# A two-layer decoder trunk on one core: the order of the output projection's blocks, of the work on VectorE between two stages, and of the first phase

## The chip, the core and the metric

The kernel runs on one core of a Trainium2 chip. The core has a matrix engine (TensorE; PE in the profile, with its weight loads on PEld), VectorE (DVE), ScalarE (ACT), GpSimd (POOL), and SyncE (SP), which here only issues DMAs. They run side by side and meet at semaphores. SBUF is the on-chip memory, and PSUM (eight banks of 128 x 512 fp32) takes the matmul results. The metric is the device time of one execution in microseconds (us), lower is better.

## The reference, cut to what matters

One sequence of 512 positions with 1024 features passes through two layers; every array is fp32.

```
c_act = silu(c)
for layer in (0, 1):
    sh_m, sc_m, g_m, sh_f, sc_f, g_f = split(c_act @ ada_w[layer] + ada_b[layer], 6)
    hm = x * (1 + sc_m) + sh_m
    y  = mixer(hm)                        # layer 0: gated linear attention + mLSTM
                                          # layer 1: stick-breaking + dilated window attention
    x  = layer_norm(RES_ALPHA * x + (1 + g_m) * y,  ln_g[layer, 0], ln_b[layer, 0])
    hf = x * (1 + sc_f) + sh_f
    yf = (silu(hf @ w1) * (hf @ w3)) @ w2
    x  = layer_norm(RES_ALPHA * x + (1 + g_f) * yf, ln_g[layer, 1], ln_b[layer, 1])

# end of layer 0's mixer
hb = sigmoid(ob) * head_norm(mlstm(...), ml_g)
y  = concatenate([oa, hb]) @ w_out        # (512 x 1024) @ (1024 x 1024)
```

## The kernel before

**Products.** A product in fp32 is made of three: each operand is split in a high part (`h_hi`, `w_hi`) and the rest (`h_lo`, `w_lo`), and PE adds up hi\*lo, hi\*hi and lo\*hi in PSUM. The weights come as slots of 128 x 1024, 512 KB each, numbered through the program: 0 to 5 the first phase, then the other projections of layer 0, 29 to 36 the output projection `out0`, 37 to 80 the up and gate projections of the first feed-forward stage `ffn0`, then its down projection, and layer 1 in the same way. SP loads slot s into `raw[s % 4]`; ACT makes `w_hi` (L738), POOL makes `w_lo` (L692), and in the first phase DVE makes it (L1862). `w_hi` and `w_lo` have four places each as well (`RING` = `RAW` = 4). ACT starts slot s when PE is done with slot s - 4 (`slot_done`), SP when POOL or DVE is done with the `w_lo` of slot s - 4. The input's high part is ACT's work (L752, L934), its low part DVE's (L1784, L2138). The high part of a chunk is made of `tmp`, which DVE (L2066, L2131) or ACT (L767) writes.

**adaLN vectors.** They are six blocks of 1024 for each layer, and run beside the products. For a block, DVE adds up eight scaled slots of `ada_w` in `ada_acc` (L1797 the first, L1800 the other seven, in `ada_block`), and PE adds over the partitions with eight matmuls one column wide (`ada_cols`). The slots come through two buffers `ada_raw`; SP issues slot i when DVE is done with slot i - 2, and `ADA_BESIDE` says behind which weight slot it does so. Block 4, the scale of ffn0's input, is wanted before ffn0 starts.

**First phase.** The shift and scale of layer 0's input come in four pieces of 256 columns (p = 0 to 3). For each, DVE adds up a part in `first_block` (L1847, L1850) and PE takes the rest itself (`FIRST_ON_PE`) and adds over the partitions (`first_cols`, L1321). DVE adds the bias (`first_mod`, L1857 and L1858), ACT scales two chunks of x (L767), and PE takes these in the products va and qa (L1332 to L1334). The whole phase loads `ada_first`, x and six weight slots.

**out0.** The concatenated input has eight chunks of 128 features: 0 to 3 of the linear attention, 4 to 7 of the mLSTM, which are last. For each of these four, ACT scales the head's numerator (L914), DVE multiplies it with the gate (`ml_gate`, L2059), PE transposes it (`turn_in`, L1501), DVE scales it into `tmp` (`cat_tmp`, L2066), ACT makes `h_hi`, DVE `h_lo` (`cat_lo`, L1784). The output has four blocks of 128 positions, two banks each; the transposes use banks 4 and 5, which are block 2's. PE does blocks 0, 3 and 1 with chunks 0 to 3, then block 2 with chunks 0 to 3, which frees the places of slots 29 to 32, then for each block in turn chunks 4 to 7 (L1131 to L1133).

**Between two stages** (`norm`). For each block DVE adds the residual (L2165, L2166), takes statistics (L2170 to L2175), and ACT normalizes (L947). PE transposes two blocks at a time into banks (`turn`, L1115), and these halves of 256 positions go chunk by chunk through `half_chunks`: DVE L2131, ACT L934, DVE L2138. The next stage's first products are done by halves: half 0 on all of a step's units, then half 1. When both halves are through, DVE also scales the normalized x with gain and bias (`affine`, L2205 and L2206, two instructions of 128 x 1024 a block), for the residual that comes later.

**ffn0** takes slots in steps of four (two of `w1`, two of `w3`). In every step DVE has the products of up and gate (L2235, then the low part of the hidden state) and two instructions on an `ada_w` slot for each of four slots of its two buffers (the loop on SP issues a weight slot and an ada slot in turn). Layer 1 opens with the projections qc and kc, whose results DVE takes out of PSUM in `qk_panel` (L2280).

Each engine runs its instructions strictly in the order in which they are written.

## Time and profile before

| | |
|---|---|
| time, median of 3 runs | 1407.68 us (1406.48 to 1409.59) |
| the profiled execution's own time | 1406.98 us |
| its span in the trace | 1405.2 us |
| PE busy | 1343.3 us (96%), 6558 matmuls |
| DVE, ACT, POOL busy | 619.5 (44%), 456.8 (33%), 507.5 (36%) |
| granted TensorE clock, mean | 0.98 |
| DMA | 173.81 MB, 124 GB/s on average, 332 GB/s in the first fortieth |

A row of the profile is one instruction or a few of one kind: start in us from the span's start, busy us, engine, line of the kernel, operation, output and inputs with their shapes, how many (x), and in brackets how long the engine stood still before it and what it waited for. Busy shares are averages over stages which differ in what they wait for.

### The profile page before, as it was taken

The page shows a single profiled execution, that of the slowest core. Times are in us where ns is not written, and L with a number is a line of the kernel's source. Part 1 is how long each engine was busy: PE and PEld are TensorE (multiplying, and loading weights), DVE is VectorE, ACT ScalarE, POOL GpSimd, SP SyncE. Part 2 cuts the span into 40 slices and gives each one's busy share as a digit, 9 for nine tenths or more (in the row PEclk, how much of TensorE's full clock was granted, in tenths as well). Part 3 has the DMA queues.
Part 4 walks back from the last instruction along what each step waited for, and adds up shares of the span by engine and source line. Part 5 has one row for each costly group of instructions (what it writes and reads, how often), then busy time and mean ns, then how long its engine had stood idle before and what let it go on. Part 6 is the DMA issues. An engine that isn't in the chain of part 4 may idle for free.

```text
span 1405.2 us, 17072 instructions
## 1 busy us (share of the span) xinstructions
PE 1343.3 (96%) x6558; PEld 1111.4 (79%) x6558; DVE 619.5 (44%) x842; ACT 456.8 (33%) x622; POOL 507.5 (36%) x209
## 2 busy tenths in 40 slices
PE   7999999889999999999899999988989999999996
PEld 6778877778888888888788777878888888887885
DVE  4489657578534343300884323347692101100006
ACT  3343254333232332112322344316243323232112
POOL 0243222323453444344235122220254444444444
PEclk9999999999999999999999899999999999999998
DMA  9972546522555465643325421112023322234312
GB/s 332 165 150 80 190 135 121 180 76 98 191 190 195 163 218 173 183 129 96 119 80 191 113 90 53 42 57 76 30 91 108 101 91 103 90 103 137 90 60 60
DMA packets 93538, 173.81 MB, mean 124 GB/s; under 512 B 15736, under 2 KB 61960, under 8 KB 93357
## 3 DMA queue, kind: packets, MB, share of 16 engines
q1 hardware_dynamic: 90344, 169.63, 39.1%
q10 hardware_dynamic: 3140, 3.43, 0.9%
q8 instruction: 39, 0.64, 0.2%
q14 instruction: 15, 0.11, 0.0%
HBM read 170.87 MB, written 4.52 MB: 125 GB/s over the span
## 4 chain that ended last, share of the span: by engine, by line
PE 68%; issue 19%; POOL 6%; DVE 4%; ACT 1%; DMA 1%; SPq 0%; POOLq 0%; DVEq 0%; ACTq 0%
PE ps L1099 13%; PE ps L1100 13%; PE ps L1101 13%; POOL w_lo L692 6%; PE ps L1131 6%; PE ps L1132 6%; PE ps L1133 6%; PE ps L1614 1%; PE ps L1274 1%; PE ps L1275 1%; PE ps L1276 1%; PE ps L1642 1%; PE ps L1625 1%; PE ps L1629 1%; PE ps L1288 1%
## 5 line engine op out<-in xcount | busy, mean ns | idle before, releaser
L692 POOL TENSOR_TENSOR w_lo<-raw,w_hi 128x1024 fp32r<-128x1024 f32 x197 | 488.3, 2484 | 857.1 <-ACT w_hi L738 856.7
L1099 PE MATMUL ps<-h_lo,w_hi 128*128 128x512 f32 (+2 forms) x1064 | 402.0, 378 | 15.1 <-DVE h_lo L2138 5.9
L1100 PE MATMUL ps<-h_hi,w_hi 128*128 128x512 f32 (+2 forms) x1064 | 398.1, 374 | 0.0
L1101 PE MATMUL ps<-h_hi,w_lo 128*128 128x512 f32 (+2 forms) x1064 | 397.8, 374 | 0.0
L738 ACT ACTIVATE w_hi<-raw 128x1024 fp32r<-128x1024 f32 x203 | 213.2, 1057 | 483.9 <-PE ps L1133 177.0
L1099 PEld LDWEIGHTS ps<-h_lo,w_hi 128*128 128x128 f32 (+1 forms) x1064 | 203.8, 192 | 55.1 <-issue 8.4
L1101 PEld LDWEIGHTS ps<-h_hi,w_lo 128*128 128x128 f32 (+1 forms) x1064 | 203.7, 191 | 35.4
L1100 PEld LDWEIGHTS ps<-h_hi,w_hi 128*128 128x128 f32 (+1 forms) x1064 | 204.2, 192 | 34.2
L2235 DVE TENSOR_TENSOR tmp<-tmp,ps 128x512 f32<-128x512 f32 x44 | 30.1, 688 | 261.4 <-PE ps L1101 261.4
L1131 PE MATMUL ps<-w_hi,hid_lo 128*128 128x512 f32 x344 | 136.8, 398 | 1.8 <-issue 0.9
L1133 PE MATMUL ps<-w_lo,hid_hi 128*128 128x512 f32 x344 | 136.8, 398 | 0.0
L1132 PE MATMUL ps<-w_hi,hid_hi 128*128 128x512 f32 x344 | 136.7, 397 | 0.0
L2165 DVE TENSOR_TENSOR ps<-ps,gate_ffn 128x1024 f32<-128x1024 f32 x7 | 8.6, 1230 | 192.2 <-PE ps L1133 192.2
L1131 PEld LDWEIGHTS ps<-w_hi,hid_lo 128*128 128x128 f32 x344 | 65.1, 189 | 18.1 <-issue 1.3
L2254 DVE SCALAR_TENSOR_TENSOR ada_acc<-ada_raw,c_act,ada_acc 128x1024 f32<-128x1024 f32 x35 | 58.3, 1666 | 44.6 <-DMA ada_raw<-astream 44.2
L1133 PEld LDWEIGHTS ps<-w_lo,hid_hi 128*128 128x128 f32 x344 | 65.0, 189 | 15.6
L1132 PEld LDWEIGHTS ps<-w_hi,hid_hi 128*128 128x128 f32 x344 | 65.0, 189 | 15.6
L1800 DVE SCALAR_TENSOR_TENSOR ada_acc<-ada_raw,c_act,ada_acc 128x1024 f32<-128x1024 f32 x35 | 62.5, 1786 | 23.7 <-DMA ada_raw<-astream 21.2
L990 ACT ACTIVATE hid_hi<-tmp 128x512 f32 (+1 forms) x44 | 27.7, 633 | 92.3 <-DVE tmp L2235 92.2
L1274 PE MATMUL ps<-w_hi,h_lo 128*128 128x512 f32 (+1 forms) x128 | 48.0, 375 | 0.0
L1275 PE MATMUL ps<-w_hi,h_hi 128*128 128x512 f32 (+1 forms) x128 | 46.9, 367 | 0.0
L1276 PE MATMUL ps<-w_lo,h_hi 128*128 128x512 f32 (+1 forms) x128 | 46.8, 366 | 0.0
(276 smaller groups left out, 1586.3 us busy)
## 6 DMA issues: line engine op xcount, KB each, us to landing
raw<-wstream SPq DMA_DIRECT2D x205, 512.0 KB, 4.0
ada_raw<-astream SPq DMA_DIRECT2D x80, 512.0 KB, 4.3
ada_first<-astream SPq DMA_DIRECT2D x16, 256.0 KB, 6.8
ada_first<-astream SPq DMA_DIRECT2D x8, 512.0 KB, 10.5
ln_rows<-row_scratch SPq DMA_DIRECT2D x3, 1024.0 KB, 6.7
skew_scratch<-f_scratch ACTq DMA_DIRECT2D x1, 2304.0 KB
xa<-xT SPq DMA_DIRECT2D x4, 512.0 KB, 8.5
out<-xa SPq DMA_DIRECT2D x3, 512.0 KB, 3.5
```

Of the source, the lines that this page charges most:

```text
L692: nc.gpsimd.tensor_tensor(w_lo[:, slot, :], raw[:, slot % RAW, :], w_hi[:, slot, :].bitcast(F32), ALU.subtract).then_inc(sem("w_lo_ready"), 1)
L738: nc.scalar.activation(w_hi[:, slot, :], raw[:, slot, :], ACT.Copy).then_inc(sem("w_hi_ready"), 1)
L1099: pe.matmul(o, w_h, x_l, start=start, stop=False)
L1100: pe.matmul(o, w_h, x_h, start=False, stop=False)
L1101: return pe.matmul(o, w_l, x_h, start=False, stop=stop)
L1131: pe.matmul(o, x_lo, w_h, start=k == 0, stop=False)
L1132: pe.matmul(o, x_hi, w_h, start=False, stop=False)
L1133: m = pe.matmul(o, x_hi, w_l, start=False, stop=k == nk - 1)
L1274: pe.matmul(o, h_lo[:, k, tokens], w_hi[:, s % RING, w], start=start, stop=False)
L1275: pe.matmul(o, h_hi[:, k, tokens], w_hi[:, s % RING, w], start=False, stop=False)
L1276: m = pe.matmul(o, h_hi[:, k, tokens], w_lo[:, s % RING, w], start=False, stop=stop)
L1800: V.scalar_tensor_tensor(ada_acc[:], src, c_act[:, k:k + 1], ada_acc[:], ALU.mult, ALU.add).then_inc(sem("ada_step"), 1)
```

## The change

- **out0.** Four more pairs of buffers hold `w_hi` and `w_lo` of slots 33 to 36, in columns of the arena that the mLSTM has left by then. PE does blocks 0, 3 and 1 with chunks 0 to 3 as before, then finishes block 0 and block 1 with chunks 4 to 7; `ada_cols(4)` follows; then block 2 with all eight chunks, the transposes of blocks 0 and 1, and block 3's chunks 4 to 7. The scheme is the one that `out1` had already, and shares its code now. ACT makes `w_hi` of slot 33 right after the scaling of the mLSTM's heads, and of 34, 35, 36 behind `h_hi` of chunks 5, 6 and 7. Slots 37 to 40 wait for places 29 to 32, which PE leaves in block 2.
- **adaLN block 4 in out0.** DVE's last four slots of it came behind all of the chunks' work; now 4 and 5 come behind `ml_gate(1)`, 6 and 7 between `cat_tmp(7)` and `cat_lo(6)`. SP issues the loads of 6 and 7 (ada slots 36 and 37 are its 4 and 5) as `ADA_BESIDE` says.
- **Norm 0 on ACT.** `w_hi` of ffn0's first slots comes before the second and third normalization.
- **Turn of half 1 before ffn0.** It stands behind the second step unit of half 0, and stood behind the first.
- **Scaling of x.** Before ffn0 and ffn1 two blocks are scaled early and two behind ffn's first step. Before layer 1 all four are scaled behind `qk_panel("kc1")`.
- **First phase.** DVE makes `h_lo` of a piece's first chunk (for p = 0) and `w_lo` of slot 1 ahead of the reduction for piece 1, and the other slots' `w_lo` behind a whole reduction. PE calls `first_cols(p + 1)` ahead of the products of chunks 1, 3 and 5, and did so between the two products of a chunk. One slot of piece 3 moves from DVE to PE.

```diff
-    FIRST_ON_PE = ((0, 1, 2, 3), (7,), (7,), ())
+    FIRST_ON_PE = ((0, 1, 2, 3), (7,), (7,), (7,))
...
-                  29: (26, 27), 30: (28, 29), 31: (30, 31), 32: (32, 33), 34: (34, 35), 36: range(36, 40)}
+                  29: (26, 27), 30: (28, 29), 31: (30, 31), 32: (32, 33), 34: (34, 35), 35: (36, 37), 36: (38, 39)}
...  ACT, out0
         hi_until(out0 + 4)
         for h in range(1, 4):
             ml_scaled(h)
+        hi_until(out0 + 5)
         for n in range(4, KC):
             hi_of_chunk(H_BASE["cat0"] + n, n)
+            if n >= 5:
+                hi_until(out0 + n + 1)
...  ACT, norm
             normalize(0)
-            normalize(1)
...
             n0 = SLOTS[following][0]
-            hi_until(n0 + 1)
+            if i == 0:
+                hi_until(n0 + 2)
+            normalize(1)
+            hi_until(n0 + (4 if i == 0 else 1))
             normalize(2)
...  PE, the first units of ffn
-                        if i == 2 and hf == 0 and q == 1 and u == 0:
+                        if i != 1 and hf == 0 and q == 1 and u == 0:
                             turn(i, 1)
-                    if i != 2 and hf == 0 and q == 0:
+                    if i == 1 and hf == 0 and q == 0:
                         turn(i, 1)
...  PE, first phase
-                if k == 5:
-                    first_cols(3)
+                if k % 2 and p < 3:
+                    first_cols(p + 1)
...
-                    if k % 2 and p < 2 and part is (first_qa if k % 4 == 3 else first_va):
-                        first_cols(p + 1)
...  PE, out0, behind blocks 0, 3 and 1 with chunks 0 to 3
-            pe.wait_ge(sem("h_tmp_ready"), H_BASE["cat0"] + KC)
-            for k in range(4):
-                rows_of(2, k).then_inc(sem("slot_done"), 1)
+        for tb in range(2):
+            for k in range(4, KC):
+                if tb == 0:
+                    slot_waits(OUT[0] + k)
+                    pe.wait_ge(sem("h_ready"), H_BASE["cat0"] + k + 1)
+                m = out_row(0, tb, k)
+            m.then_inc(sem("y_full"), 1)
+        pe.wait_ge(sem("r_ready"), 1)
+        ada_cols(4, 1)
+        pe.wait_ge(sem("h_tmp_ready"), H_BASE["cat0"] + KC)
+        for k in range(KC):
+            m = out_row(0, 2, k)
+            if k < 4:
+                m.then_inc(sem("slot_done"), 1)
+        m.then_inc(sem("y_full"), 1)
+        turn(0, 0)
+        for k in range(4, KC):
+            out_row(0, 3, k).then_inc(sem("slot_done"), 1)
...  DVE, norm and ffn
-            for tb in range(TB):
+            early = 0 if i == 1 else 2
+            for tb in range(early):
                 affine(tb, ln_rows2, sem("x_row"))
...
+            def rest():
+                for tb in range(early, TB):
+                    affine(tb, ln_rows2, sem("x_row"))
...
             step(0, True)
+            rest()
...
         qk_panel("kc1")
+        rest1()
```

Below, rows of instructions stand as the two programs have them, one engine at a time.

DVE in the first phase, before: from the first piece's bias (L1857) to the second's. L1847 and L1850 are the reduction, L1784 is `h_lo`, L1862 `w_lo`.

```order
L1857 TENSOR_TENSOR mod<-ps,vec 128x2
L1858 TENSOR_TENSOR scl<-ps,scale_b_74 128x2
L1847 TENSOR_SCALAR ada_acc<-ada_first,c_act 128x512
L1850 SCALAR_TENSOR_TENSOR ada_acc<-ada_first,c_act,ada_acc 128x512
L1784 TENSOR_TENSOR h_lo<-tmp,h_hi 128x512
L1862 TENSOR_TENSOR w_lo<-raw,w_hi 128x1024
L1850 SCALAR_TENSOR_TENSOR ada_acc<-ada_first,c_act,ada_acc 128x512
L1784 TENSOR_TENSOR h_lo<-tmp,h_hi 128x512
L1850 SCALAR_TENSOR_TENSOR ada_acc<-ada_first,c_act,ada_acc 128x512 x2
L1862 TENSOR_TENSOR w_lo<-raw,w_hi 128x1024
L1850 SCALAR_TENSOR_TENSOR ada_acc<-ada_first,c_act,ada_acc 128x512 x2
```

DVE there, after (L1873 the bias, L1863 and L1866 the reduction, L1800 `h_lo`, L1878 `w_lo`):

```order
L1873 TENSOR_TENSOR mod<-ps,vec 128x2
L1874 TENSOR_TENSOR scl<-ps,cols 128x2
L1800 TENSOR_TENSOR h_lo<-tmp,h_hi 128x512
L1878 TENSOR_TENSOR w_lo<-raw,w_hi 128x1024
L1863 TENSOR_SCALAR ada_acc<-ada_first,c_act 128x512
L1866 SCALAR_TENSOR_TENSOR ada_acc<-ada_first,c_act,ada_acc 128x512 x2
L1800 TENSOR_TENSOR h_lo<-tmp,h_hi 128x512
L1866 SCALAR_TENSOR_TENSOR ada_acc<-ada_first,c_act,ada_acc 128x512 x4
L1878 TENSOR_TENSOR w_lo<-raw,w_hi 128x1024
```

Two instructions of the reduction stood between the scale and the first `h_lo`, and one more between two of the `w_lo`s; now nothing stands ahead of the first `h_lo`, and the reduction for the next piece begins behind the first `w_lo`.

DVE in out0, before: from `ml_gate(0)` (L2059) to the last of block 4 (L1800). L2066 is `cat_tmp`, L1784 `cat_lo`.

```order
L2059 TENSOR_TENSOR og<-og,num 128x4x128 x2
L2066 TENSOR_SCALAR tmp<-ps,vec 128x512
L2059 TENSOR_TENSOR og<-og,num 128x4x128
L2066 TENSOR_SCALAR tmp<-ps,vec 128x512
L2059 TENSOR_TENSOR og<-og,num 128x4x128
L1784 TENSOR_TENSOR h_lo<-tmp,h_hi 128x512
L2066 TENSOR_SCALAR tmp<-ps,vec 128x512
L1784 TENSOR_TENSOR h_lo<-tmp,h_hi 128x512
L2066 TENSOR_SCALAR tmp<-ps,vec 128x512
L1784 TENSOR_TENSOR h_lo<-tmp,h_hi 128x512 x2
L1800 SCALAR_TENSOR_TENSOR ada_acc<-ada_raw,c_act,ada_acc 128x1024 x4
```

DVE there, after (L2074 `ml_gate`, L1816 block 4, L2081 `cat_tmp`, L1800 `cat_lo`):

```order
L2074 TENSOR_TENSOR og<-og,num 128x4x128 x2
L1816 SCALAR_TENSOR_TENSOR ada_acc<-ada_raw,c_act,ada_acc 128x1024 x2
L2081 TENSOR_SCALAR tmp<-ps,vec 128x512
L2074 TENSOR_TENSOR og<-og,num 128x4x128
L2081 TENSOR_SCALAR tmp<-ps,vec 128x512
L2074 TENSOR_TENSOR og<-og,num 128x4x128
L1800 TENSOR_TENSOR h_lo<-tmp,h_hi 128x512
L2081 TENSOR_SCALAR tmp<-ps,vec 128x512
L1800 TENSOR_TENSOR h_lo<-tmp,h_hi 128x512
L2081 TENSOR_SCALAR tmp<-ps,vec 128x512
L1816 SCALAR_TENSOR_TENSOR ada_acc<-ada_raw,c_act,ada_acc 128x1024 x2
L1800 TENSOR_TENSOR h_lo<-tmp,h_hi 128x512 x2
```

Two instructions of block 4 stand ahead of the first `cat_tmp` now, and two ahead of the last two `cat_lo`.

DVE at the start of layer 1, before: the last two scalings of x (L2205, L2206), then the eviction of qc (L2280).

```order
L2205 TENSOR_TENSOR xa<-xa,ln_rows_79 128x8x128
L2206 TENSOR_TENSOR xa<-xa,ln_rows_79 128x8x128
L2205 TENSOR_TENSOR xa<-xa,ln_rows_79 128x8x128
L2206 TENSOR_TENSOR xa<-xa,ln_rows_79 128x8x128
L2223 MEMSET cols 128x1
L2280 TENSOR_SCALAR qc<-ps 128x512 x2
L2285 COPY f_rows<-ps 4x1152
L1806 TENSOR_TENSOR mod<-ps,vec 128x8
L1797 TENSOR_SCALAR ada_acc<-ada_raw,c_act 128x1024
```

DVE there, after: the last low parts of the input (L2154), the eviction of qc and kc (L2303), block 10's sums and those of the next (L1822, L1813, L1816), then the scaling (L2221, L2222).

```order
L2154 TENSOR_TENSOR h_lo<-tmp,h_hi 128x256 x3
L2303 TENSOR_SCALAR qc<-ps 128x512 x2
L2308 COPY f_rows<-ps 4x1152
L1822 TENSOR_TENSOR mod<-ps,vec 128x8
L1813 TENSOR_SCALAR ada_acc<-ada_raw,c_act 128x1024
L1816 SCALAR_TENSOR_TENSOR ada_acc<-ada_raw,c_act,ada_acc 128x1024 x3
L2303 TENSOR_SCALAR kc<-ps 128x512
L1816 SCALAR_TENSOR_TENSOR ada_acc<-ada_raw,c_act,ada_acc 128x1024 x4
L2303 TENSOR_SCALAR kc<-ps 128x512
L2221 TENSOR_TENSOR xa<-xa,ln_rows_78 128x8x128
L2222 TENSOR_TENSOR xa<-xa,ln_rows_78 128x8x128
L2221 TENSOR_TENSOR xa<-xa,ln_rows_78 128x8x128
```

All eight instructions of the scaling stood ahead of qc's eviction (six of them above the rows shown here or at their start), and stand behind kc's now.

## Rows read from the trace of the kernel before

**Rows 1.** A stretch: width; busy us PE, PEld, DVE, ACT, POOL; clock, DMA, GB/s.

```profile
1100.00:1150.00 50.00, 50.00 (x222) 41.42 (x221) 5.34 (x8) 15.60 (x20) 21.56 (x9) 1.00 0.33 105
```

**Rows 2.** Stretch 0 to 35, and instructions in time order: start, busy, engine, [idle].

```profile
0.00:35.00 35.00, 24.57 (x104) 21.42 (x105) 17.42 (x30) 11.99 (x15) 0.20 (x4) 1.00 0.98 332
...
15.45 0.63 ACT L752 ACTIVATE h_hi<-tmp 128x512 fp32r<-128x512 f32 x1
...
16.25 0.49 DVE L1847 TENSOR_SCALAR ada_acc<-ada_first,c_act 128x512 f32<-128x512 f32 x1 [1.68 <-DMA ada_first<-astream]
...
18.18 0.79 PE L1332 MATMUL ps<-w_hi,h_lo 128*128 128x512 f32 x1 [3.88 <-DVE h_lo L1784]
...
32.26 0.50 PE L1332 MATMUL ps<-w_hi,h_lo 128*128 128x512 f32 x1 [1.07 <-DVE h_lo L1784]
...
48.61 1.02 PE L1321 MATMUL ps<-ones,ada_acc 128*128 128x1 f32 x8 [1.97 <-DVE ada_acc L1850]
```

**Rows 3.** The timeline of out0 on ACT, POOL and PE.

```profile
262.13 1.06 ACT L738 ACTIVATE w_hi<-raw 128x1024 fp32r<-128x1024 f32 x1 [3.09 <-PE ps L1133]
...
263.26 9.01 POOL L692 TENSOR_TENSOR w_lo<-raw,w_hi 128x1024 fp32r<-128x1024 f32 x3 [14.19 <-ACT w_hi L738]
...
269.08 0.47 PE L1131 MATMUL ps<-w_hi,h_lo 128*128 128x512 f32 x1 [1.58 <-issue]
...
272.38 0.47 PE L1131 MATMUL ps<-w_hi,h_lo 128*128 128x512 f32 x1 [1.67 <-issue]
...
274.70 0.47 PE L1131 MATMUL ps<-w_hi,h_lo 128*128 128x512 f32 x1 [0.70 <-issue]
...
290.28 1.86 PE L1115 MATMUL ps<-cst,xa 128*128 128x128 f32 x15 [1.10 <-ACT xa L947]
```

**Rows 4.** The timeline of ACT, DVE and POOL in out0 and behind it.

```profile
246.87 4.35 ACT L914 ACTIVATE num<-num,cols,rstd 128x128 f32<-128x128 f32 x11
...
248.17 1.45 DVE L2059 TENSOR_TENSOR og<-og,num 128x512 f32<-128x512 f32 x1 [1.50 <-ACT num L914]
...
259.68 1.28 DVE L1800 SCALAR_TENSOR_TENSOR ada_acc<-ada_raw,c_act,ada_acc 128x1024 f32<-128x1024 f32 x1
...
264.30 2.45 DVE L1800 SCALAR_TENSOR_TENSOR ada_acc<-ada_raw,c_act,ada_acc 128x1024 f32<-128x1024 f32 x1 [1.96 <-DMA ada_raw<-astream]
...
312.40 1.45 DVE L2131 TENSOR_SCALAR tmp<-ps,scl,bia 128x256 f32<-128x256 f32 x3 [1.99 <-PE ps L1115]
...
312.72 2.39 POOL L692 TENSOR_TENSOR w_lo<-raw,w_hi 128x1024 fp32r<-128x1024 f32 x1 [4.72 <-ACT w_hi L738]
...
313.77 1.62 DVE L2138 TENSOR_TENSOR h_lo<-tmp,h_hi 128x256 fp32r<-128x256 f32 x1
```

**Rows 5.** The start of ffn0 on PE, and the stretch in which its clock was halved.

```profile
299.71 0.39 PE L1099 MATMUL ps<-h_lo,w_hi 128*128 128x256 f32 x1 [2.09 <-DVE tmp L2131]
...
302.76 0.58 PE L1099 MATMUL ps<-h_lo,w_hi 128*128 128x256 f32 x1 [2.05 <-DVE h_lo L2138]
...
303.00:307.00 4.00, 4.00 (x19) 3.93 (x20) 3.97 (x10) 1.99 (x4) 2.36 (x1) 0.50 0.77 262
...
311.75 0.44 PE L1115 MATMUL ps<-cst,xa 128*128 128x128 f32 x2 [1.47 <-ACT xa L947]
```

**Rows 6.** DVE and PE around the second step of ffn0.

```profile
330.71 0.40 PE L1099 MATMUL ps<-h_lo,w_hi 128*128 128x512 f32 x1
...
338.75 0.75 DVE L2257 TENSOR_SCALAR ada_acc<-ada_raw,c_act 128x1024 f32<-128x1024 f32 x1
...
348.09 0.47 PE L1099 MATMUL ps<-h_lo,w_hi 128*128 128x512 f32 x1 [0.87 <-POOL w_lo L692]
```

**Rows 7.** The start of layer 1 on DVE and PE, and the stretch behind it.

```profile
725.31 0.69 DVE L2280 TENSOR_SCALAR qc<-ps 128x512 f32<-128x512 f32 x1
...
726.10 0.76 PE L1099 MATMUL ps<-h_lo,w_hi 128*128 128x512 f32 x1 [2.27 <-issue]
...
726.00:730.00 4.00, 3.90 (x9) 3.13 (x10) 3.86 (x5) 0.00 (x0) 0.00 (x0) 0.50 0.09 24
```

153 lines of the change are left out of this document (76 added, 77 removed).

## The prediction, made before the changed kernel was run

> **What bounds the kernel now.** I read the page's first part, then windows of 50 us, then the list of waits of PE, then PE's timeline at every pause. PE is busy for 96% of the span, and in a stretch between two stages without a pause: 222 matmuls of 512 columns in 50.00 us, or 0.225 us each, at the full clock, while DVE has 5.34 us of work and POOL 21.56 [rows 1]. Other engines matter only where PE stands still, so each edit is worth what it does to one of PE's pauses. Those within its reach are three in the first phase [rows 2], four in out0 [rows 3], three at the start of ffn0 [rows 5], one a step later [rows 6], and one at the start of layer 1 [rows 7]. Two of these twelve are followed by a stretch at a granted clock of 0.50, the lower of TensorE's two levels (1.2 against 2.4 GHz) [rows 5, 7].
>
> **First phase.** PE's first product waits 3.88 us, for a `h_lo` [rows 2]. ACT has the high part ready at 15.45 + 0.63 = 16.08, but DVE has a reduction ahead, and that waits 1.68 us for its DMA until 16.25. In the new order `h_lo` comes first: 16.08 + 0.69 + 0.1 to start, so PE begins at 16.9 instead of 18.18, a gain of 1.3. The waits of 1.07 and 1.97 [rows 2] are of the same kind (the second is for the last piece's reduction on DVE, which is one instruction shorter and is asked for no earlier than before), and I take both away. PE pays for four more tiny products of its own and their weight loads, some 0.8 by the eight of 48.61 at 1.02 us. Sum: -1.3 - 1.1 - 2.0 + 0.8 = -3.5. Bounds: the DMA is at 0.98 of its time here, 332 GB/s [rows 2]. If the pieces land only when DVE took them, the waits of 1.07 and 1.97 come back under another name and only the start is left, -1.3 + 0.8, with part of one wait about -1.0. If the four small products are free, -4.1. I take -3.5: both waits name DVE as the releaser, and not the DMA.
>
> **out0: what goes.** PE waits 1.58, 1.67 and 0.70 for `w_lo` of slots 34 to 36. ACT can't begin them before places 29 to 32 are free at 262.13, and POOL then takes three at 3.0 each [rows 3]. With buffers of their own they don't wait for PE. The 1.10 ahead of the transposes [rows 3] waits for the normalized block 1. Block 1 is now done a whole block (48 matmuls, 10.9 us) ahead of these, so it goes. Together 5.05.
>
> **out0: what comes.** I lay DVE's new order on the old times. `ml_gate(1)` ends at 248.17 + 1.45 = 249.6. Slots 4 and 5 of block 4, 1.28 each [rows 4], last until 252.2. ACT is through with the heads at 246.87 + 4.35 = 251.2 and makes `w_hi` of slot 33, so POOL is busy from 252.4 to 254.8. Here the trace shows how the two engines meet: a DVE instruction with two inputs in SBUF stands still while POOL works. `h_lo` of 128 x 256 took 1.62 at 313.77, to just behind the end of POOL's (312.72 + 2.39 = 315.11), and a block 4 instruction 2.45 in place of 1.28. The three with a PSUM input beside that same POOL instruction took 1.45 together, 0.48 each, and were not held [rows 4]. The Trainium skill has this as a rule ("SBUF — State Buffer", "SBUF: two separate sides"): the shared port pair is an exclusive lock for the whole instruction, and with two SBUF inputs VectorE needs it. By that rule the extra wait below comes; were the ports shared evenly, DVE would be through about 5 us sooner and there would be none.
> With that, and 0.7 for `cat_tmp` or `cat_lo` (the like eviction of 128 x 512 took 0.69 [rows 7]): `cat_tmp(4)` to 252.9, `ml_gate(2)` held to 255.4, `cat_tmp(5)` 256.2, `ml_gate(3)` 256.9, `cat_lo(4)` 257.5, `cat_tmp(6)` 258.3. POOL takes slot 34 from 258.0 to 260.4, so `cat_lo(5)` ends at 261.0 and `cat_tmp(7)` at 261.8. Slot 35 goes from 261.0 to 263.4; block 4's slot 6 is held and ends at 264.7, then POOL has slot 36 until 267.1, slot 7 ends at 268.3, and `cat_lo(6)` at 269.0.
> PE is through with chunks 0 to 3 of three blocks at about 261.6 (1.0 later than now, since the last transpose waits for `ml_gate(3)`), does chunks 4 and 5 of block 0 (six matmuls, 1.36 us each), and wants chunk 6 at 264.3. It waits 4.8. I add 2.1 for a stretch at the lower clock behind so long a pause: behind 2.27 and behind 2.09 and 2.05 the clock was 0.50 for four us and more [rows 5, 7], where each us holds half of the work. Sum: +6.9 - 5.05 = +1.9. Bounds: no wait at all, -5.05; one more of POOL's splits in DVE's way, 2.4, a wait of 7.2 and the clock, +4.3. The moved DMAs cost nothing: ada slots 36 to 39 are issued one weight slot sooner, with their landings ahead of the times above. The four `w_hi` are on ACT between chunks, 1.06 each, and ACT was idle for 3.09 there [rows 3].
>
> **ffn0's start.** Today 2.09, 2.05 and 1.47 [rows 5]. The first two come of splits that lie among the chunks of half 0: POOL holds `h_lo`, and ACT has a `w_hi` between two `h_hi`. Now these four slots are split before the second and third normalization. The four us from 303 at clock 0.50 did the work of two [rows 5], and go with them: -2.0. So 7.6 goes. In its place PE comes earlier to the transposes of half 1, which want the last normalized block: a wait of about 1.4, like the 1.47 now. The chunks' own pace (one `tmp` and one `h_lo`, 0.48 + 0.41, against 1.36 per chunk on PE, but with the first two in a row) costs 0.7. Net -5.5; bounds -8.3 (none of the new waits) and 0 (all come back, since DVE arrives late from out0).
> **A step later** PE waits 0.87 for slot 44 [rows 6]. SP's loop issues weight and ada slots in turn, and the ada slot needs DVE. DVE's first of block 5 ends at 339.5, 8.8 behind the start of PE's second step at 330.71 [rows 6]. Now DVE has step 0 at once, 2.6 us, then four scalings, at least 1.28 each and one or two held by POOL for another 1.2, so that it is 10.1 behind: +1.3. Bounds 0 to 2.5. What the six instructions taken away ahead of step 0 give is nothing, as PE didn't wait for them.
> The wait for chunk 6 pushes everything, so from out0 to slot 44 it is +1.9 - 5.5 + 1.3 = -2.3.
>
> **Layer 1's start.** PE waits 2.27 at 726.10 since bank by bank it needs qc out of PSUM, which DVE does at 725.31 [rows 7], behind eight scalings of x at 1.2 us or more. They go behind kc now: -2.3. If the clock of 0.50 behind it (3.90 us of four [rows 7]) stays up too, -4.4. If something else of DVE's is as late, 0. I take -2.3, since a chunk pause before it can drop the clock as well. The scalings meet POOL's splits later and delay the eviction of vc by some 0.5, for which nobody waits for long. Norm 2 and ffn1 have no pause of this kind, the loop of POOL unrolled around slot 33 has the same instructions, so both are 0.
>
> **The sum**: -3.5 - 2.3 - 2.3 = -8.1, on the profiled execution's 1406.98 (1.8 of it outside the span of 1405.2, which stay): 1398.9. The median is 0.7 higher, so 1399.6.
>
> **Rivals.**
> A. *No wait in out0.* DVE's last low parts come in time, because POOL's splits start later or earlier than I have them and miss the long instructions. For: the hold is an accident of a few tenths. Against: the two instructions of block 4 are 2.6 us even unheld, ahead of a chunk wanted in 2.7. Price: -6.9 and some of the one at slot 44 back: about 1393.
> B. *The first phase is bound by its DMAs.* For: 0.98 busy [rows 2]. Against: of the waits only DVE's own was for a DMA. Price: the first phase gives 1.0 instead of 3.5: 1402.
> C. *Little changes.* The new wait in out0 is at its upper bound (+4.3 for +1.9), and half of what ffn0 wins comes back: 1399.6 + 2.4 + 2.8 = 1404.8, and up to 1408 if layer 1's start gives nothing.
> D. *Slower.* SP's queue in ffn0: each weight slot is behind an ada slot that waits for DVE, and DVE takes step j only when PE has done it. If DVE is late once, the weights are late, PE is late and nothing makes up for it. This decides when DVE's first of block 5 ends more than about 11 us behind the start of the second step: then a split as late as slot 44's, 2.5 a time, comes in each of five turns, +12, to 1411. For: the 0.87 is there [rows 6], and it gets worse. Against: behind it DVE has waited for its DMAs, not they for it.
>
> **How the numbers follow.** Forecast 0.50, A 0.20, B 0.15, C 0.10, D 0.05. The forecast's own range is 1396 to 1402.5. The range for 8 in 10 takes in most of A, all of B, and the lower part of C: 1391.5 to 1404.5. The measurement tells 0.2% (2.8 us) from no change: faster is below 1404.9, which is the forecast, A, B and half of C, 0.85 with a little off for what I haven't seen; same 0.10; slower, D, 0.05.
>
> **What would show it.** First phase: PE's first product at 16.9 and no pause up to out0; a pause whose releaser is a DMA speaks for B. out0: no wait for `w_lo` of 34 to 36, but one of 4 to 5 us ahead of block 0's third late chunk, with `h_lo` as releaser, two instructions of block 4 of about 2.4 in front of it, and the clock down behind it. ffn0: half 0 without a pause of 2 us and at clock 1.0; about 2.2 at slot 44. Layer 1: qc's eviction some 9 us earlier. The forecast is wrong if PE goes through out0 without a pause (A), or if the mean wait of ffn0's later steps is not zero (D).

## The result, and the profile after

The changed kernel takes 1387.72 us (median of 4 runs, 1384.56 to 1391.53), the kernel before 1408.47 beside it. The ratio is 0.9851, 95% interval 0.9836 to 0.9867: 20.8 us faster. The forecast was 1399.6, 8.1 faster, with a range down to 1391.5, so the measured time lies below the range. The direction was right, the size was wrong by more than a factor of two.

The profiled execution has a span of 1382.7 us; it is the fastest of the four. These are the places that the forecast named, in PE's timeline (start, busy, engine, in brackets the pause ahead and what it waited for):

```profile
16.63 0.80 PE L1340 MATMUL ps<-w_hi,h_lo 128*128 128x512 f32 x1 [2.55 <-DVE h_lo L1800]
...
23.91 1.05 PE L1329 MATMUL ps<-ones,ada_acc 128*128 128x1 f32 x8 [0.76 <-DVE ada_acc L1866]
...
263.33 0.76 PE L1546 MATMUL ps<-out_hi,h_lo 128*128 128x512 f32 x1 [3.86 <-DVE h_lo L1800]
...
338.77 0.47 PE L1114 MATMUL ps<-h_lo,w_hi 128*128 128x512 f32 x1 [1.56 <-POOL w_lo L695]
...
710.55 0.80 PE L1114 MATMUL ps<-h_lo,w_hi 128*128 128x512 f32 x1
```

The 3.88 of the first product is 2.55 now [rows 2]. The pauses of 1.07 and 1.97 are gone, with one of 0.76 in their place. In out0 the three for `w_lo` and the 1.10 [rows 3] are gone, and 3.86 stands ahead of block 0's third late chunk. Between it and 338.77, where three stood [rows 5], the timeline has 0.17 and 0.27. At slot 44 there is 1.56 for 0.87 [rows 6], and the last row, the counterpart of 726.10 [rows 7], has no pause.

Here are three windows of the changed kernel and two of the one before (columns: busy us of PE, PEld, DVE, ACT, POOL with their instructions, then PE's clock, the DMAs' share, GB/s). The first of before and of after lie in down0, the second in down1, the third of after in ffn1. After:

```profile
570.00:620.00 50.00, 50.00 (x222) 41.42 (x221) 1.60 (x4) 9.54 (x9) 23.10 (x10) 1.00 0.53 110
1290.00:1340.00 50.00, 50.00 (x222) 41.40 (x221) 0.00 (x0) 9.54 (x9) 22.61 (x10) 1.00 0.27 85
1100.00:1150.00 50.00, 50.00 (x222) 41.42 (x221) 5.34 (x8) 14.63 (x18) 22.81 (x10) 1.00 0.30 95
```

Before:

```profile
570.00:620.00 50.00, 50.00 (x215) 40.23 (x215) 7.89 (x7) 9.56 (x9) 21.50 (x10) 1.00 0.56 147
1290.00:1340.00 50.00, 50.00 (x216) 40.25 (x216) 0.00 (x0) 9.55 (x9) 21.24 (x9) 1.00 0.32 95
```

This is the surprise. PE is busy without a pause at the full clock in all five, and still does 215 or 216 matmuls in the down projections of before and 222 in those of after, as many as everywhere else [rows 1]. From the start of one matmul to the start of the next it is 0.2333 us in the one and 0.2267 in the other.

Where the time went in the two profiled executions, by the start of the same matmul in both:

| up to the end of | before | after | this stage, after less before |
|---|---|---|---|
| first phase | 73.61 | 68.95 | -4.7 |
| layer 0's mixer up to out0 | 241.29 | 236.71 | +0.1 |
| out0, start of ffn0, up to slot 44 | 348.09 | 338.77 | -4.7 |
| ffn0 | 559.55 | 550.27 | 0.0 |
| down0 | 686.56 | 672.52 | -4.8 |
| norm 1 and qc | 726.10 | 710.55 | -1.5 |
| layer 1's mixer, out1 | 1021.64 | 1001.83 | -4.3 |
| ffn1 | 1267.92 | 1248.18 | +0.1 |
| down1, end | 1405.2 | 1382.7 | -2.7 |

The forecast had the first, third and sixth line, 8.1 in all; they hold 10.9. It had 0 for down0, layer 1's mixer and down1, and these hold 11.8.

### The profile page after: what moved, and what is told of

It is laid out like the page before. It is cut to its first block, busy times and chain, and to the rows that moved or that the text cites. A ratio compares the mean times of both kernels' runs of the same rounds, so it can differ in the third digit from the quotient of the medians.

```text
span 1382.7 us, 17078 instructions
## 1 busy us (share of the span) xinstructions
PE 1332.4 (96%) x6566; PEld 1109.4 (80%) x6566; DVE 615.0 (44%) x841; ACT 457.4 (33%) x622; POOL 507.3 (37%) x209
## 4 chain that ended last, share of the span: by engine, by line
PE 81%; issue 7%; DVE 7%; POOL 3%; ACT 2%; DMA 0%; DVEq 0%; SPq 0%; POOLq 0%; ACTq 0%
PE ps L1114 15%; PE ps L1115 15%; PE ps L1116 14%; PE ps L1146 5%; PE ps L1148 5%; PE ps L1147 5%; POOL w_lo L695 2%; PE ps L1282 2%; PE ps L1283 2%; PE ps L1284 2%; PE ps L1643 1%; PE ps L1671 1%; PE ps L1296 1%; PE ps L1250 1%; PE ps L1252 1%
## 5 line engine op out<-in xcount | busy, mean ns | idle before, releaser
L695 POOL TENSOR_TENSOR w_lo<-raw,w_hi 128x1024 fp32r<-128x1024 f32 x193 | 477.5, 2480 | 826.7 <-ACT w_hi L747 826.4
L747 ACT ACTIVATE w_hi<-raw 128x1024 fp32r<-128x1024 f32 x199 | 208.9, 1057 | 486.3 <-DMA raw<-wstream 167.2
L1148 PE MATMUL ps<-w_lo,hid_hi 128*128 128x512 f32 x344 | 133.9, 389 | 0.0
L1147 PE MATMUL ps<-w_hi,hid_hi 128*128 128x512 f32 x344 | 133.8, 389 | 0.0
L2278 DVE SCALAR_TENSOR_TENSOR ada_acc<-ada_raw,c_act,ada_acc 128x1024 f32<-128x1024 f32 x35 | 58.9, 1684 | 44.8 <-DMA ada_raw<-astream 44.5
L1816 DVE SCALAR_TENSOR_TENSOR ada_acc<-ada_raw,c_act,ada_acc 128x1024 f32<-128x1024 f32 x35 | 57.4, 1639 | 24.1 <-DMA ada_raw<-astream 21.5
L1283 PE MATMUL ps<-w_hi,h_hi 128*128 128x512 f32 (+1 forms) x128 | 46.7, 365 | 0.0
L1284 PE MATMUL ps<-w_lo,h_hi 128*128 128x512 f32 (+1 forms) x128 | 46.7, 365 | 0.0
```

Of the source, the lines that this page charges most:

```text
L695: nc.gpsimd.tensor_tensor(w_lo[:, slot, :], raw[:, slot % RAW, :], w_hi[:, slot, :].bitcast(F32), ALU.subtract).then_inc(sem("w_lo_ready"), 1)
L747: nc.scalar.activation(w_hi[:, slot, :], raw[:, slot, :], ACT.Copy).then_inc(sem("w_hi_ready"), 1)
L1147: pe.matmul(o, x_hi, w_h, start=False, stop=False)
L1148: m = pe.matmul(o, x_hi, w_l, start=False, stop=k == nk - 1)
L1283: pe.matmul(o, h_hi[:, k, tokens], w_hi[:, s % RING, w], start=False, stop=False)
L1284: m = pe.matmul(o, h_hi[:, k, tokens], w_lo[:, s % RING, w], start=False, stop=stop)
```

## The experiments

Times are medians in us. The kernel before ran beside every one of these kernels and took 1407.0 to 1408.7; the ratio is to it, with a 95% interval. A difference to the changed kernel is one of medians, to its 1387.72 where nothing else is said. The interval given with some of them is worked out from both ratios.

**Where the arena lies.** The arena is the part of SBUF, laid out last, in which `hid`, the hidden state of the feed-forward stages, and the mixers' buffers lie. The change puts the vector `scale_b1`, 32 bytes per partition that lay ahead of the arena, in free columns of `cols`, and so moves all of the arena from byte 137120 to 137088:

```diff
-    scale_b1 = at("scale_b1", [P, KC])
...
+    scale_b1 = cols[:, 5, 0:KC]
```

Two kernels turn that one thing.

```diff
+    place[0] += 32
     arena = place[0]
```

In the kernel before:

> The kernel before with 32 unused bytes ahead of the arena, so that its start goes from 137120 (32 above a multiple of 64) to 137152 (a multiple of 64); no instruction is moved. Theory 'place': the change dropped a 32-byte vector ahead of the arena and so put hid_hi and hid_lo, the stationary tiles of the down projections, on multiples of 64 bytes; that alone takes the matmul spacing of down0 and down1 from 0.2333 us to 0.2268, 528 matmuls each, 6.9 us in all, and perhaps a few us more in layer 1, whose tensors lie in the arena too: 6 to 12 us faster than before. Rival 'order': the spacing is a consequence of the new order (other engines' work beside the down projections), and then this kernel keeps 0.2333 and stays within 0.2% of before.

1407.73, ratio 0.9994 (0.9984 to 1.0004), spacing 0.2333. In the changed kernel:

> The changed kernel with 32 unused bytes ahead of the arena, which puts its start back at 137120. Theory 'place': spacing in the down projections 0.2333 again, and the time some 7 to 12 us over the changed kernel's 1387.7, about 1395 to 1399; what is left against before is what the new order brings, by the pauses of the trace 4.7 in the first phase, 4.7 from out0 to slot 44 and about 1 at layer 1's start. Rival 'order': the spacing stays 0.2268 and the time stays at 1387 to 1389.

1393.73, ratio 0.9901 (0.9879 to 0.9922), spacing 0.2333 again:

```profile
570.00:620.00 50.00, 50.00 (x216) 40.24 (x215) 2.27 (x5) 9.15 (x10) 21.77 (x9) 1.00 0.51 119
```

So it is the place and not the order: no instruction differs from the changed kernel, and it costs 6.0 us (interval 3 to 11). But it is not multiples of 64, as the kernel before with the pad shows. The next three look for the rule. The first moves hid, the stationary operand of the down projections (the one that is loaded as weights), by 8 columns, the second the arena by 96 bytes, and the third hid by 24 columns.

```diff
-    hid_hi = ar("hid_hi", [P, FC, S], 0, F32R)
-    hid_lo = ar("hid_lo", [P, FC, S], FC * S, F32R)
+    hid_hi = ar("hid_hi", [P, FC, S], 8, F32R)         # 24 and 56 in others
+    hid_lo = ar("hid_lo", [P, FC, S], FC * S + 8, F32R)
```

> The kernel before with hid_hi and hid_lo alone set 8 columns (32 bytes) further on in the arena, so that only they lie on multiples of 64 bytes. Theory 'stationary tile': the down projections go at 0.2268 and the gain is their 6.9 us. Rival 'whole arena': part of the gain of the first run comes from other tensors (the attention of layer 1, the evictions into the arena); then this one gains clearly less than that. Rival 'order': no gain.

1408.30, ratio 1.0004 (0.9991 to 1.0016).

> The kernel before with 96 unused bytes ahead of the arena: its start goes from 137120 to 137216, a multiple of 128, where 137152 (a multiple of 64 only) had brought nothing. The changed kernel's arena starts at 137088, a multiple of 128 too. Theory 'place, by 128': the down projections' matmul spacing goes from 0.2333 us to 0.2267, 528 in each of two stages, 6.9 us, and the kernel is 0.4 to 0.6% faster than before with no instruction moved. Rival 'absolute place': it is the arena's lower start, or how it stands to another tensor, and this one stays at 0.2333 and at the time of before.

1408.07, ratio 0.9989 (0.9974 to 1.0005), 0.2333 in down0 and 0.2323 in down1.

> The kernel before with only hid_hi and hid_lo 24 columns (96 bytes) further on, which puts these two on a multiple of 128. Theory 'stationary tile': spacing 0.2267 in the down projections and the same gain as with the whole arena moved. Rival 'more than hid': no change of spacing, or a gain clearly smaller than that of the moved arena.

1407.07, ratio 0.9988 (0.9972 to 1.0004), 0.2324 in both. With the first pad these are four misses: remainders of 192 (twice) and 0 (twice) of 256 are as slow as before's 160, or nearly. A remainder of 128 was left:

> The kernel before with hid_hi and hid_lo 56 columns (224 bytes) further on: their start is 137344, which leaves 128 when divided by 256. So far the slow starts were 137120, 137152 and 137216 (remainders 160, 192 and 0), and the fast ones 137088 in the changed kernel and 32896 of h_hi, the stationary tiles of ffn's neighbour out0 (remainder 128 both). Theory 'remainder 128 of 256': spacing in the down projections 0.2267 and 0.3 to 0.5% faster than before, with no instruction moved. Rival 'something else of the changed arena': 0.2333 and no gain.

1402.62, ratio 0.9956 (0.9942 to 0.9970), down0 and down1 as in the changed kernel:

```profile
570.00:620.00 50.00, 50.00 (x223) 41.38 (x222) 8.78 (x8) 10.53 (x10) 22.20 (x9) 1.00 0.65 165
1290.00:1340.00 50.00, 50.00 (x222) 41.39 (x222) 0.00 (x0) 9.54 (x9) 22.25 (x10) 1.00 0.30 95
```

That is 6.1 us from 224 bytes per partition, with no instruction moved. `w_hi`, the moving operand there, and `h_hi`, the stationary one of out0 and the moving one of ffn0, lie at 82048 and 32896, remainder 128 both. Is it each place, or one against the other? For that `w_hi` and `w_lo`, and with them all that lies behind, are moved by 128 bytes:

```diff
+    place[0] += 128
     w_hi = at("w_hi", [P, RING, SLOT], F32R)
```

> The kernel before with 128 unused bytes ahead of w_hi (w_hi, w_lo and all behind them 128 bytes further on: w_hi at 82176, remainder 0 of 256) and hid_hi and hid_lo 24 columns further on in the arena, at 137344 (remainder 128). The moving operand w_hi and the stationary operand then differ by 128 in the remainder. Theory 'absolute place of the stationary tile': spacing 0.2267 in the down projections. Rival 'place of the two operands against each other': 0.2333 there, and in out0, where h_hi (remainder 128) is stationary and w_hi moves, over 0.2267 as well. Rival 'neither' as in the run before: 0.2333 in the down projections only.

> The kernel before with w_hi and w_lo 128 bytes further on (remainder 0 of 256) as in the run that went at 0.2325 everywhere, and with hid_hi and hid_lo at 137472, remainder 0 too. Theory 'the same remainder': the down projections go at 0.2267, and ffn (w at 0, h at 128) at 0.2325. Rival 'each at 128 by itself': 0.2325 or 0.2333 in both.

The first took 1422.73 in its one run, the second 1415.70 in its one. Their windows in ffn0 and down0 follow. For comparison, ffn0 in the kernel before:

```profile
400.00:450.00 50.00, 50.00 (x230) 41.67 (x229) 21.97 (x21) 13.61 (x17) 19.84 (x8) 1.00 0.49 172
```

With `w_hi` at remainder 0 and hid at 128:

```profile
400.00:450.00 50.00, 50.00 (x225) 40.89 (x224) 17.84 (x18) 14.02 (x17) 21.39 (x9) 1.00 0.48 168
590.00:640.00 50.00, 50.00 (x216) 40.51 (x216) 1.60 (x4) 9.54 (x9) 21.40 (x10) 1.00 0.52 121
```

With hid at remainder 0, like `w_hi`:

```profile
400.00:450.00 50.00, 50.00 (x225) 40.84 (x225) 18.74 (x18) 14.14 (x17) 22.26 (x10) 1.00 0.47 168
590.00:640.00 50.00, 50.00 (x222) 41.44 (x221) 1.61 (x4) 9.55 (x9) 22.64 (x10) 1.00 0.52 113
```

Down0 is back at 222 matmuls with both operands at 0. In ffn0, where `w_hi` at 0 meets h at 128, a matmul of 512 columns comes every 0.2324 us in both, and every 0.2269 in the kernel before (some one-column matmuls stand in these windows too). So what counts is whether stationary and moving operand start at the same remainder of 256 bytes.

The changed kernel's own out0 agrees. Of its four new pairs of buffers that of slot 33 begins at remainder 128, like `h_hi`, and the high parts of slots 34 to 36 at 192. In block 2, at the full clock, the six matmuls with slot 33 (from 281.47 on) start 0.2266 us apart, those with slot 34 0.2322, with 35 0.2288 and with 36 0.2303. With the pad of 32 bytes the six of slot 33 are at 0.2334 as well. Two things are open: why 64 bytes cost less here than in down0, and why hid at 137216 gave 0.2333 in down0 with the arena moved and 0.2324 with hid alone moved.

**The first phase undone** in the changed kernel (`FIRST_ON_PE`, the place of `first_cols` and DVE's order as in the diff's minus lines).

> The changed kernel with the first phase of before (the slots on PE, the place of first_cols, the order on DVE). The forecast priced the new first phase at 3.5 us, the profiles of before and after show 4.7 by the start of the linear attention: so 3.5 to 4.7 us slower than the changed kernel. Rival: a start that is late by 4 is swallowed later, since the pauses behind it depend on DMAs and not on PE: under 1.5.

1393.03, ratio 0.9886 (0.9856 to 0.9916): 5.3 over the changed kernel (interval 0.2 to 9.7), and the three pauses are back:

```profile
17.87 0.79 PE L1340 MATMUL ps<-w_hi,h_lo 128*128 128x512 f32 x1 [3.48 <-DVE h_lo L1802]
...
31.47 0.50 PE L1340 MATMUL ps<-w_hi,h_lo 128*128 128x512 f32 x1 [1.05 <-DVE h_lo L1802]
...
47.80 1.02 PE L1329 MATMUL ps<-ones,ada_acc 128*128 128x1 f32 x8 [1.93 <-DVE ada_acc L1868]
```

They were DVE's and not the DMAs', which ends rival B. The traces narrow the price. From PE's first product to its short wait for `w_lo` at the start of the next stage (67.96 before, 63.30 after) it is 46.7 to 47.0 us in all nine profiles with the new first phase, and 49.6 to 51.5 in all eleven with the old one. The long ones among these are seven in which the clock is at 0.50 for 3.4 us behind the third pause. The old order in the changed kernel is one of the seven, the kernel before is not.

**Layer 1's scaling undone**:

```diff
-            early = 0 if i == 1 else 2
+            early = 4 if i == 1 else 2
```

> The changed kernel with all four scalings of x ahead of layer 1's first projections, where they stood before. The forecast gave their move 2.3 us (0 to 4.4). The wait of 2.27 ahead of the second projection's first matmul comes back, and the time is about 2 us over the changed kernel's, 1389.7. Rival: 0, since qc's eviction waits for something else now; or 4.4 with a stretch at clock 0.50.

1392.08, ratio 0.9883 (0.9869 to 0.9898): 4.4 more (interval 1.5 to 7.5). The pause is back:

```profile
716.12 0.76 PE L1114 MATMUL ps<-h_lo,w_hi 128*128 128x512 f32 x1 [2.11 <-issue]
```

The 2.3 of the forecast lies inside. In the trace the stretch from the last wait for a normalized block (687.05 in the changed kernel) to the wait for `sb_a` in the mixer (777.60) is 92.0 us here for 90.5 in the changed kernel, so the pause itself is worth about 1.5.

**Norm 0 undone**, with out0 kept:

```diff
-            if i == 0:
-                hi_until(n0 + 2)
             normalize(1)
-            hi_until(n0 + (4 if i == 0 else 1))
+            hi_until(n0 + 1)
...
-                        if i != 1 and hf == 0 and q == 1 and u == 0:
+                        if i == 2 and hf == 0 and q == 1 and u == 0:
...
-            early = 0 if i == 1 else 2
+            early = (4, 0, 2, 2)[i]
```

> The changed kernel with norm 0 as before (order of w_hi and normalization on ACT, transposes of half 1 behind the first unit, all four scalings of x ahead of ffn0's first step), and with out0 as changed. The forecast gave this place 5.5 us, and the profile of the changed kernel shows no pause there. If norm 0's order brings it, the pauses of 2.09, 2.05 and 1.47 come back, and the time is 4 to 7 us over the changed kernel's, about 1393. Rival: out0's new order brings it, since slots 37 to 40 get their places earlier and block 1 its normalization; then the time rises by under 2 us.

1396.72, ratio 0.9906 (0.9890 to 0.9922): 9.0 more (interval 4.6 to 10.9). Two of the three pauses are back, one larger:

```profile
300.61 0.39 PE L1112 MATMUL ps<-h_lo,w_hi 128*128 128x256 f32 x1 [2.08 <-DVE h_lo L2152]
...
309.59 0.65 PE L1128 MATMUL ps<-cst,xa 128*128 128x128 f32 x2 [3.15 <-ACT xa L959]
```

From the start of out0 to the end of ffn0 (236.71 to 547.56 in the changed kernel, 239.49 to 555.24 here) it is 4.9 us more. The rest lies elsewhere, mostly in half-clock stretches, and isn't shown to be a price of this order.

**Out0 alone.** The changed kernel with the three undone parts together and the arena's 32 bytes back, so that against before only out0 is new (and two of ffn1's scalings).

> The changed kernel with the old first phase, the old norm 0, the old scaling ahead of layer 1 and the arena back at 137120: against the kernel before, only out0's new order with its four buffers is left (and two of ffn1's scalings behind its first step). By the forecast +1.9 us in out0 itself, by the sum of the single parts (5.3 + 9.0 + 4.4 + 6.0 = 24.7 against 20.8 in all) +4: slower than before by 1 to 4 us, 1410 to 1413. Rival: out0 brings something by itself (ffn0's slots split earlier), 3 to 6 us faster than before, and the parts do not add up because two of them take away the same pause.

1409.29, ratio 0.9997 (0.9981 to 1.0013): no difference that can be told. Four pauses of 5.05 together are gone, and one of 3.82 is there with a half-clock stretch of 1.6 behind it, and ffn0's start has pauses of 2.08 and 3.16 where before has three of 5.61 together:

```profile
270.29 0.47 PE L1547 MATMUL ps<-out_hi,h_lo 128*128 128x512 f32 x1 [3.82 <-DVE h_lo L1801]
```

**The wait in out0.**

```diff
-        ada_block(4, False, range(6, KC))
         cat_lo(6)
         cat_lo(7)
+        ada_block(4, False, range(6, KC))
```

> The changed kernel with adaLN block 4's slots 6 and 7 on DVE behind the last two low parts of out0's input, where all four stood before, and not ahead of them. By the forecast's step the low part of chunk 6 is late because these two instructions and POOL's splits alternate on DVE: the wait of 3.86 us at 263.33 should shrink to under 1.5 and the clock of 0.50 behind it (2.2 us) should go, 3 to 5 us faster than the changed kernel, about 1383.5. Rival: ada_cols(4) and the scale of ffn0's input then come late and the wait turns up ahead of ffn0 or at the sums of block 4, no gain.

1385.80, ratio 0.9826 (0.9807 to 0.9845), 1.9 under the changed kernel (interval 0 to 7) where 3 to 5 were expected. The pause is 0.85, and the clock stays up behind it:

```profile
263.70 0.47 PE L1546 MATMUL ps<-out_hi,h_lo 128*128 128x512 f32 x1 [0.85 <-DVE h_lo L1800]
```

In its own stage the gain is plain. From the start of out0 (the wait for `og` at 237.69 in the changed kernel) to slot 44 it is 101.1 and 100.8 us in the two profiles of the changed kernel, and 95.3, 95.5 and 95.5 in the three with slots 6 and 7 behind (this kernel and the two profiles of the faster version below).

With slots 4 and 5 behind as well:

> The changed kernel with all four slots 4 to 7 of adaLN block 4 behind the last low part of out0's input, as before. Slots 6 and 7 behind took the wait from 3.86 to 0.85; with 4 and 5 behind as well the 0.85 should go too, 1 us under that kernel's 1385.8 unless the sums of block 4 (ada_cols) come late: then a new wait of 1 to 3 us ahead of block 2, and 1386 to 1388.

1392.96, ratio 0.9896 (0.9875 to 0.9917), 5 us slower than the changed kernel. The pause in the late chunks doesn't go (1.15). I had foreseen a new wait ahead of block 2, of 1 to 3 us; it is 4.38, on the column matmuls of `ada_cols(4)`, with the clock at 0.50 from 273.4 to 283.6. Its releaser is DVE's first residual, which stands behind all four slots, and two of these wait for their loads (2.02 and 1.49 us).

```profile
274.67 1.65 PE L1296 MATMUL ps<-cst,ada_acc 128*128 128x1 f32 x7 [4.38 <-DVE xa L2181]
```

So slots 4 and 5 are needed ahead, and 6 and 7 are not needed between.

**A faster version**, with slots 6 and 7 behind, and the transposes of half 1 ahead of layer 1 one slot later, behind the third slot of half 0. There the changed kernel has them ahead of ffn0: the "second step unit" of the section on the change is two slots, and they stand behind its first.

> A try at a faster version: the changed kernel with slots 6 and 7 of block 4 behind, and with the transposes of half 1 ahead of layer 1 behind the third unit of half 0, as the changed kernel has them ahead of ffn0. The wait of 1.5 to 1.9 for the normalized block ahead of layer 1 should go: 1 to 2 us under 1385.8. If the wait only moves to half 1's first chunk, the same time.

1384.20, ratio 0.9826 (0.9805 to 0.9847); the pause for the normalized block ahead of layer 1 is gone, with one of 0.40 for `w_lo` in its place. The ratio is that of the kernel with slots 6 and 7 behind alone, so a gain from the transposes isn't shown. On one chip with the changed kernel:

> The changed kernel once more, on the chip of the next run. If the half-clock stretches at unchanged pauses vary by execution, its profile will show another set of them (49.6, 172, 547.5 or 780 for some) and a span over 1382.7, though no instruction differs; the median stays at 0.985 of before. If they are fixed by the program, the set is the same as in its first profile.

> The changed kernel with slots 6 and 7 of block 4 behind and the transposes ahead of layer 1 one unit later, beside the changed kernel on the same chip. By its pauses (3.0 less in out0, 1.9 less ahead of layer 1) 2 to 5 us under the changed kernel. If the earlier difference was chance, the two agree within 1 us.

The changed kernel took 1386.68, ratio 0.9854 (0.9836 to 0.9872), the other 1383.96, ratio 0.9836 (0.9810 to 0.9862). It beats the kernel before clearly. Against the changed kernel its median is 3.5 and 2.7 us lower, but the intervals overlap, so that is likely and not shown.

**The clock where nothing changed.** Half-clock stretches stand in both profiles at places that the change does not touch. The kernel before is started later:

```diff
+        for q in range(2):
+            sp.dma_start(ada_raw[:, 0, :], astream[0]).then_inc(sem("late"), 16)
+            sp.wait_ge(sem("late"), 16 * q + 16)
         sp.dma_start(vec[:], vecs).then_inc(sem("in_vec"), 16)
```

> The kernel before with two extra loads of 512 KB ahead of its first load, each waited for, so that everything starts some 6 to 9 us later. Theory 'clock by the pause alone': the same pauses (0.87 at 559.55, 1.33 at 794.43 and the others) are followed by the same half-clock stretches, and the time is that of before plus the delay. Rival 'clock by where it falls': the same pauses come elsewhere, some of the stretches (1.5 us at 559.9, 2.0 at 777.5, 1.8 at 798.6) go or new ones come, as in the changed kernel, and the time is off the sum by 1 to 4 us.

1417.39, ratio 1.0059 (1.0038 to 1.0081): 8.9 over before. In the profiled execution the first product came 7.3 later (25.45 for 18.18), and the stretches at ffn0's start, behind ffn0 and in layer 1 are the same set as in before, each 9.6 to 9.7 us later. That speaks for the pause alone. Two more stretches, at 57.8 and 184.5 (1.4 and 1.2 us lost), which before's profile has not, make up for the rest of its span's 9.7. They are not the delay's: with nothing but buffers moved in the kernel before (the arena by 96 bytes, hid by 24 or 56 columns) they are there too.

The second profile of the changed kernel speaks against the pause alone: the same program has a stretch at 171 that its first profile has not. First execution, then second:

```profile
170.00:174.00 4.00, 4.00 (x24) 3.47 (x24) 2.64 (x14) 1.37 (x2) 0.26 (x1) 1.00 0.01 4
```

```profile
171.00:175.00 4.00, 4.00 (x12) 3.17 (x12) 2.64 (x14) 1.28 (x2) 0.17 (x1) 0.57 0.02 4
```

Behind the pause of 0.87 at ffn0's end, which every version has, the clock of before is down and that of the changed kernel is not. Before, then after:

```profile
559.50:563.50 4.00, 3.95 (x10) 3.12 (x11) 3.90 (x4) 0.02 (x1) 2.93 (x1) 0.57 0.46 154
```

```profile
550.00:554.00 4.00, 3.73 (x16) 3.08 (x17) 3.90 (x6) 0.24 (x1) 2.96 (x1) 1.00 0.47 147
```

It is down there in all ten profiles of the kernel before, its variants and out0 alone, and in six of the ten of the changed kernel and its other variants. Where it is down, it is 138.4 us from this pause to the last wait for a normalized block behind down0, and 136.8 where it is not (the changed kernel and its variants without the pad). The faster version's two profiles, one program, differ as well: one takes 148.8 us from the wait for `sb_a` in layer 1's mixer to the wait for `lg_loc`, with a stretch at 0.50, the other 145.6 without. Nor is a pause needed: the stretches from 775.0 in before and from 709.0 in after begin while PE works without one, on a run of one-column matmuls and the six or eight behind it that use 33 or 64 of the array's 128 rows (`sel_sb`, and `qc` with `kc`). What decides it was not settled.

## Why the prediction was wrong

**The step that failed** is the one that says that only PE's pauses matter ("Other engines matter only where PE stands still, so each edit is worth what it does to one of PE's pauses"). PE without a pause at the full clock was taken for PE at its best, from a window in ffn1 [rows 1]. A window in down0 would have shown 215 matmuls in place of 222. The lines that take `scale_b1` from ahead of the arena got no term in the sum, and no reason for it. Their effect was measured in two ways: 6.0 us (the pad in the changed kernel) and 6.1 us (hid moved in the kernel before, ratio 0.9956). The spacing gives nearly the same: 528 matmuls in each of two stages times 0.0066 are 7.0. With the measured 6.0 the forecast would have been 1393.6.

That leaves 5.9 of the 11.9 us by which the measured time lies under the forecast. By the profiles 1.2 of it are in the first phase and 2.4 from out0 to slot 44; the rest can't be told from half-clock stretches that one execution has and another has not. The parts undone one by one come to 5.3 + 9.0 + 4.4 + 6.0 = 24.7 with nothing for out0, against 20.8 in all; their intervals are wide enough for that. The bound of -8.3 at ffn0's start is a slip: without the two new waits it is -7.6.

**First phase**: right in mechanism, a little small. -3.5 against -4.7 in the profile and -5.3 by undoing it. The first product came at 16.63 (16.9 forecast) and both waits went, with 0.76 coming. What was left out is the clock. Matmuls spaced 0.43 us, the lower level, lasted from 18.8 to 23.9 before and from 17.2 to 19.4 after. How soon the clock rises differs by execution: 2.9 us behind the first product here, 4.2 to 5.4 behind it in the other eight profiles with the new first phase, 4.0 to 5.9 in those with the old. The stage's length hardly follows it (46.7 to 47.0 us with the new order), since the pause of 0.76 is missing where the clock rises later. The half-clock stretch behind the third pause, in seven of eleven profiles of the old order and in none of the new, was left out too.

**Out0**: right in mechanism, and the best worked part. The chain on DVE, with POOL's splits (its making of `w_lo`) in its way, ended within 1.3 us of the forecast's. These are the last scaling and the low parts, then POOL's splits, of the changed kernel:

```profile
256.72 5.87 DVE L1816 SCALAR_TENSOR_TENSOR ada_acc<-ada_raw,c_act,ada_acc 128x1024 f32<-128x1024 f32 x2
262.50 1.28 DVE L1800 TENSOR_TENSOR h_lo<-tmp,h_hi 128x512 fp32r<-128x512 f32 x2
```

```profile
252.99 5.23 POOL L716 TENSOR_TENSOR out_lo<-raw,out_hi 128x1024 fp32r<-128x1024 f32 x2 [2.90 <-ACT out_hi L738]
258.50 3.00 POOL L716 TENSOR_TENSOR out_lo<-raw,out_hi 128x1024 fp32r<-128x1024 f32 x1 [0.28 <-ACT out_hi L738]
```

Two instructions of 1.28 us took 5.87: the first, 2.58 us long, ran beside the second split, and the second, 3.18 long, beside the third. The low part of chunk 6 was ready at 263.1; the forecast had 269.0 on before's times, which are 4.6 later here, so 264.4. The wait was 3.86 for 4.8, and the half-clock stretch 2.2 for 2.1. Net +1.0 by these for +1.9; alone, out0's new order made no difference that can be told (interval -2.7 to +1.8 us). A pause of 0.43 for the last gated head, at 251.95, came with it. The forecast cites the Trainium skill's page "SBUF — State Buffer", section "SBUF: two separate sides", for an exclusive lock between VectorE and GpSimd. This trace agrees: the extra wait came, and the two instructions took 5.87 us.

**Ffn0's start**: right in mechanism. All three pauses went. Of the two new waits that I had put in (1.4 and 0.7) there are 0.27 and 0.17, and slot 44 cost 0.7 more and not 1.3. From the start of out0 to slot 44 it was -4.7 for -2.3. Undone by itself norm 0 is worth 4.9 in the profile. The forecast's -5.5 + 1.3 = -4.2 is near that. So the step that was mis-sized here is the pair of new waits, 2.1 us for 0.4.

**Layer 1's start**: the pause of 2.27 went as forecast, but the clock was down all the same (matmuls spaced 0.43 us up to 715.8): it had fallen at 709.0, with PE at work without a pause on matmuls of one column and then on six of 33 rows:

```profile
706.02 1.84 PE L1296 MATMUL ps<-cst,ada_acc 128*128 128x1 f32 x16
707.79 2.82 PE L1626 MATMUL ps<-sel_sb,rel_sb 33*4 33x384 f32 x6
```

By the profiles the region gave 1.5, and undoing it costs 1.5 in the trace and 4.4 in the medians (interval 1.5 to 7.5); 2.3 lies in it, and 1.5 is the better figure.

**Down0**, forecast 0, gave 4.8, and not all of it is the arena's place. 1.6 are the half-clock stretch behind the pause at ffn0's end, which this execution of the changed kernel lacks. The spacing's share is 3.1: from the pause at ffn0's end to the last wait for a normalized block it is 139.9 us in the changed kernel with the pad and 136.8 without, both without that stretch. In down1 the pad costs 3.0.

**Layer 1's mixer**, forecast 0, gave 4.3 in these two executions. 3.2 of it are the half-clock stretch at 795.5, which comes and goes between the two profiles of one program, as shown above, and 1.3 lie between 726 and 794, where before has a stretch from 775.0 that is twice as long as its counterpart in after (6.8 and 3.4 us). That is luck of these two executions as far as the traces tell. The stretch at 795.5 is missing in six of the ten profiles of the changed kernel and its variants and in two of the other ten; whether the change makes it rarer isn't shown. The medians agree with some of it being chance: the spans differ by 22.5, the medians by 20.8.

**Rivals.** A did not come (the wait is there), B fell with the first phase undone, C and D did not come: ffn0 behind slot 44 takes 211.5 us in both kernels. That the place of a buffer could be the largest single term was no rival, and the range was too narrow at the fast end for it.

## What to carry to other kernels

Count matmuls per us in every stage that looks fully busy, not in one: down0 was 100% busy at the full clock and still 3% slow. When a change frees or adds a buffer, work out which others it moves, and compare the addresses of the operands that meet on PE. Before long instructions of DVE and POOL are put side by side, lay them on a common time line: that forecast a wait of 3.86 us as 4.8. And before a difference between two profiles in a stage that the change does not touch is explained, look whether two executions of one program differ there as much.
